# First norm of a fused three-mixer kernel: raw rows of x turned and split before the norm's factor is known, the factor applied later

## What is computed

```python
def rms_norm(x, gain):
    y = x32 * lax.rsqrt(jnp.mean(x32 * x32, axis=-1, keepdims=True) + RMS_EPS)
    return (y * gain).astype(x.dtype)

mem_n = rms_norm(mem, mem_norm_gain)
hn = rms_norm(x, g[0])
# mlstm_mixer(hn, ...)
proj = h @ w_in
q, k, v, o, gates = jnp.split(proj, ...)
gates = ML_GATE_CAP * jnp.tanh((gates + b_gate) / ML_GATE_CAP)
ig, lf = gates[..., :H], jax.nn.log_sigmoid(gates[..., H:])
...
num = einsum(s, v) + inter * (C @ q)
den = sum(s) + inter * (n . q)
h_out = num / max(abs(den), exp(-m_t))
hs = rms_norm(h_out, head_gain)
out = (hs * sigmoid(o)) @ w_out
```

## Time and profile before

| what | us |
|---|---|
| median of three runs (1288.68 to 1290.69) | 1288.76 |
| the profiled execution | 1288.84 |
| its span | 1287.1 |
| PE busy | 1273.9 |
| DVE busy | 890.5 |
| ACT busy | 695.2 |
| POOL busy | 118.0 |

### The profile page before, as it was taken

How to read it: one execution, slowest core, us unless ns; L and a number is a source line. 1 busy time by engine, 2 the same in 40 slices (tenths; PEclk the granted TensorE clock), 3 DMA queues, 4 the chain that set the end, 5 groups by cost and what they waited for, 6 DMA issues and landing times.

```text
span 1287.1 us, 17765 instructions
## 1 busy us (share of the span) xinstructions
PE 1273.9 (99%) x7337; PEld 1105.9 (86%) x7337; DVE 890.5 (69%) x1053; ACT 695.2 (54%) x976; POOL 118.0 (9%) x178
## 2 busy tenths in 40 slices
PE   7999999999999999999999999999999999999999
PEld 7888898988888988889888888898887888888887
DVE  4657775766666776877676666767785566887775
ACT  5755554644444656565554444565565654655443
POOL 7200100100000100030100000101330003100000
PEclk9999999999999999999999999999999999999999
DMA  8754644555555554354455565563544435465552
GB/s 267 261 164 145 201 162 131 184 193 196 196 193 183 182 163 132 132 176 152 152 178 195 196 196 192 168 197 99 164 163 138 157 134 194 138 214 184 187 194 98
DMA packets 156113, 223.64 MB, mean 174 GB/s; under 512 B 6103, under 2 KB 107635, under 8 KB 156032
## 3 DMA queue, kind: packets, MB, share of 16 engines
q1 hardware_dynamic: 154240, 218.18, 51.4%
q0 software_dynamic: 1664, 4.27, 1.0%
q10 hardware_dynamic: 128, 0.05, 0.0%
HBM read 221.44 MB, written 1.05 MB: 173 GB/s over the span
## 4 chain that ended last, share of the span: by engine, by line
PE 95%; DVE 2%; ACT 1%; POOL 1%; DMA 1%; issue 0%; SPq 0%; ACTq 0%
PE ps L443 18%; PE ps L496 10%; PE ps L497 10%; PE ps L498 10%; PE ps L445 9%; PE ps L426 5%; PE ps L428 5%; PE ps L427 5%; PE ps L678 5%; PE ps L680 5%; PE ps L679 5%; PE ps L517 1%; PE ps L984 1%; PE ps L461 1%; DVE wlo L1803 1%; DMA raw<-in_ml_w_in 1%
## 5 line engine op out<-in xcount | busy, mean ns | idle before, releaser
L1221 ACT ACTIVATE whi<-raw 128x1024 fp32r<-128x1024 f32 x411 | 424.4, 1052 | 314.2 <-PE ps L443 155.2
L1803 DVE TENSOR_TENSOR wlo<-raw,whi 128x1024 fp32r<-128x1024 f32 x408 | 489.2, 1229 | 140.1 <-ACT whi L1221 137.6
L443 PE MATMUL ps<-RR,whi 128*128 128x512 f32 x1024 | 354.0, 396 | 0.5 <-DVE wlo L1803 0.5
L445 PE MATMUL ps<-RR,wlo 128*128 128x256 f32 x1024 | 264.8, 279 | 0.1
L496 PE MATMUL ps<-whi,RR 128*128 128x512 f32 x592 | 236.5, 400 | 0.3 <-DVE wlo L1803 0.3
L497 PE MATMUL ps<-wlo,RR 128*128 128x512 f32 x592 | 230.9, 390 | 0.0
L498 PE MATMUL ps<-whi,RR 128*128 128x512 f32 x592 | 230.9, 390 | 0.0
L443 PEld LDWEIGHTS ps<-RR,whi 128*128 128x128 f32 x1024 | 184.9, 188 | 36.2 <-DVE wlo L1803 0.8
L445 PEld LDWEIGHTS ps<-RR,wlo 128*128 128x128 f32 x1024 | 193.0, 188 | 11.8 <-DVE RR L1834 0.4
L426 PE MATMUL ps<-RR,whi 128*128 128x256 f32 x512 | 147.1, 287 | 0.6 <-DVE RR L1834 0.5
L428 PE MATMUL ps<-RR,wlo 128*128 128x256 f32 x512 | 144.8, 283 | 0.0
(11 more groups left out here) (358 smaller groups left out, 1335.9 us busy)
## 6 DMA issues: line engine op xcount, KB each, us to landing
raw<-in_ffn_w_gate_up SPq DMA_DIRECT2D x44, 1024.0 KB, 5.1
raw<-in_ffn_w_down SPq DMA_DIRECT2D x33, 1024.0 KB, 4.9
raw<-in_w_in SPq DMA_DIRECT2D x28, 1024.0 KB, 5.0
raw<-in_ffn_w_up SPq DMA_DIRECT2D x22, 1024.0 KB, 5.1
raw<-in_xa_w_kv SPq DMA_DIRECT2D x16, 1024.0 KB, 5.2
raw<-in_sb_w_qkv SPq DMA_DIRECT2D x12, 1024.0 KB, 5.1
raw<-in_ml_w_in SPq DMA_DIRECT2D x11, 1024.0 KB, 5.7
raw<-in_xa_w_q SPq DMA_DIRECT2D x8, 1024.0 KB, 5.1
```

Of the source, the lines that this page charges most:

```text
L443: m = pe.matmul(two(ps[:, bank, :]), p.hi[:, k, :], XT2[:, k, :, :], start=k == 0, stop=k == 7)
L445: pe.matmul(ps[:, bank, 0:256], p.lo[:, k, :], X.h[:, k, :], start=False, stop=False)
L1221: act.activation(p.hi, p.raw, ACT.Copy).then_inc(S["w_hi"], 2 if p.n == pool_piece.n + 1 else 1)
L1803: dve.tensor_tensor(p.lo, p.raw, p.hi.bitcast(F32), ALU.subtract).then_inc(S["w_lo"], 2 if p.n in (2, late_piece.n + 1) else 1)
```

## The change

Raw x is turned as soon as it has landed, and the turned tiles (times the norm's gain) are split without the factor r. The projections q, k, v, o and the gates then lack r of their position. r is put in later:

- gate rows: r is turned into a row by two matmuls against the identity (bank 5), copied (`xrs`), and multiplied onto the gate rows; the bias goes into the tanh, divided by 15 (`gb15`).
- values: the copies out of PSUM are scaled by `x_rr` = r squared (r of the key, r of the value), the sigmoid of o has r as its scale, and the column of ones beside the values becomes r.
- the factor r of q is in the numerator and the denominator alike and drops out, so the bound exp(-m) is multiplied by `x_ir` = 1/r, which POOL makes as r times (mean + eps).

Pieces 0 and 1 are now halves of mlq0's rows (four feature tiles of all 256 columns each) and are loaded so, in packets twice as large. POOL casts their high parts in four halves, DVE subtracts them (`first_lo`) between the low tiles, and TensorE takes them in four quarters (`first_rows`). TensorE runs 8 products of zeros ahead of everything and 6 behind the transposes (`spin`). ACT's `squares(0)` moves behind pieces 2 and 3. DVE's `normed(0)` is gone. POOL's factors stand behind its four casts and wait for the later squares.

```diff
-            X = norm_rows(0)
-            pe.wait_ge(S["n_lo"], 2)
-            fm("mlq0", X, 4)
+            pe.wait_ge(S["w_zero"], 1)
+            spin(8)
...
+            pe.wait_ge(S["x_in0"], 16)
+            pe.wait_ge(S["x_in1"], 16)
+            for k in range(8):
+                b, half = half_bank(k, (0, 1, 2, 3))
+                for t in range(NT):
+                    m = pe.transpose(ps[:, b, 256 * half + 128 * t:256 * half + 128 * t + 128],
+                                     xr[:, t, 128 * k:128 * k + 128], ident[:, :])
+                m.then_inc(S["n_T"], 1)
+            spin(6)
+            X = Rows(XTh, XTl, S["n_lo"], [k + 1 for k in range(8)])
+            first_rows("mlq0", X, 4)
             fm("mlq1", X, 1)
+            pe.wait_ge(S["n_r"], 2)
+            for t in range(NT):
+                m = pe.matmul(ps[:, 5, 128 * t:128 * t + 128], x_r[t].to_broadcast([128, 128]), ident[:, :], start=True, stop=True)
+            m.then_inc(S["ml_r"], 1)
             gate_rows("mlg", X, 2)
...
@@ scalar_program
-            squares(0)
-            hi_to(2)
             act.wait_ge(S["gains"], 1)
             norm_hi(0, gain1(0, 0))
             hi_to(4)
+            squares(0)
...
@@ vector_program
+            def first_lo(n):
+                p, k = pieces[n // 2], slice(2 * (n % 2), 2 * (n % 2) + 2)
+                dve.wait_ge(S["hi_pool"], n + 1)
+                dve.tensor_tensor(p.lo[:, k, :], p.raw[:, k, :], p.hi[:, k, :].bitcast(F32), ALU.subtract).then_inc(S["lo_first"], 1)
+            dve.memset(Vx[:, 0, 0:256], 0.0).then_inc(S["w_zero"], 1)
             gain_columns(0)
-            normed(0)
-            lo_to(2)
-            norm_lo(0, gain1(0, 0))
+            norm_lo(0, gain1(0, 0), range(3))
+            first_lo(0)
+            norm_lo(0, gain1(0, 0), range(3, 4))
+            first_lo(1)
+            norm_lo(0, gain1(0, 0), range(4, 6))
+            first_lo(2)
+            norm_lo(0, gain1(0, 0), range(6, 8))
+            first_lo(3)
+            dve.wait_ge(S["lo_first"], 4)
             lo_to(4)
...
             for g, dst in ((32, fg), (0, ig)):
-                dve.wait_ge(S["dve_step"], step(dve.tensor_scalar(dst, ps[g:g + 4, 2, 0:256], gb[g:g + 4, 0:1], None, ALU.add)))
-                dve.tensor_tensor(dst, ps[64 + g:68 + g, 2, 0:256], dst, ALU.add).then_inc(S["ml_u"], 1)
+                dve.wait_ge(S["dve_step"], step(dve.tensor_copy(dst, ps[g:g + 4, 2, 0:256])))
+                dve.wait_ge(S["dve_step"], step(dve.tensor_tensor(dst, ps[64 + g:68 + g, 2, 0:256], dst, ALU.add)))
+                dve.tensor_tensor(dst, dst, xrs, ALU.mult).then_inc(S["ml_u"], 1)
...
@@ gpsimd_program
             pool.wait_ge(*at("mhalf", 1))
+            for p, sem in zip(pool_pieces, ("w_first", "w_raw0")):
+                pool.wait_ge(S[sem], 16)
+                for k in (0, 2):
+                    pool.tensor_copy(p.hi[:, k:k + 2, :], p.raw[:, k:k + 2, :]).then_inc(S["hi_pool"], 1)
             norm(0)
-            second = pieces[1]
-            pool.wait_ge(S["w_hi"], 2)
-            pool.tensor_tensor(second.lo, second.raw, second.hi.bitcast(F32), ALU.subtract).then_inc(S["lo_first"], 1)
+            pool.wait_ge(S["n_r"], 2)
+            for t in range(NT):
+                pool.tensor_tensor(x_rr[t], x_r[t], x_r[t], ALU.mult).then_inc(S["x_rr"], 1)
+            for t in range(NT):
+                pool.tensor_tensor(x_ir[t], x_r[t], n_st[0][t][1], ALU.mult).then_inc(S["x_ir"], 1)
             pool.affine_select(identb[:, :], identb[:, :], [[-1, 128]], ALU.not_equal, 1.0, base=0,
                                channel_multiplier=1).then_inc(S["identb"], 1)
...
             mem_norm(0)
-            pool.memset(V4[:, :, :, 256:257], 1.0).then_inc(S["v_ones"], 1)
+            for t in range(NT):
+                pool.tensor_copy(V4[:, t, :, 256:257], x_r[t].unsqueeze(1).to_broadcast([128, 4, 1])).then_inc(S["v_ones"], 1)
+            pool.wait_ge(*at("ml_em", 1))
+            pool.wait_ge(*at("x_ir", 2))
+            for t in range(NT):
+                e = emc[:, 8 * t + 4:8 * t + 8]
+                pool.tensor_scalar(e, e, x_ir[t], None, ALU.mult).then_inc(S["ml_ems"], 1)
```

More of the change, by code:

```diff
@@ L238, in build_program @@
         W = I["ml_w_in"][0]
-        fm_block("mlq", W, 0, 2)
+        chunk("mlq0", W[:, 0:256], "s")
+        chunk("mlq1", W[:, 256:512], "c")
         chunk("mlg", W[:, 3072:3080], "g")
@@ L294, in end @@
             return C[name].end
-        pool_piece = C["u2_0"].pieces[0]
+        pool_pieces = pieces[0:2] + C["u2_0"].pieces[0:1]
         late_piece = C["g2_1"].pieces[1]
@@ L332, in build_program @@
         sq = reg(9488, 512)
+        xrs = Vx[0:4, 1, 512:768]
+        gb15 = stat(2)
+        x_r = [n_st[0][t][2] for t in range(NT)]
+        x_rr, x_ir = [stat(1) for t in range(NT)], [stat(1) for t in range(NT)]
         rows = reg(7696, 1792).rearrange("p (n t) -> p n t", t=256)
@@ L417, in fm_piece @@
                 o = ps[:, bank, 256 * i:256 * i + 256]
[L418 to L421, removed]
+                pe.wait_ge(S["w_lo"], p.n + 1)
                 for k in range(8):
@@ L429, in fm_piece, with first_rows @@
                 m.then_inc(S["w_used"], 1)
+            def first_rows(name, X, bank):
+                for i, p in enumerate(C[name].pieces):
+                    for k0 in (0, 2):
+                        pe.wait_ge(S["lo_first"], 2 * i + k0 // 2 + 1)
+                        for c in range(2):
+                            o, r = ps[:, bank, 256 * c:256 * c + 256], slice(128 * c, 128 * c + 128)
+                            for k in (k0, k0 + 1):
+                                n = 4 * i + k
+                                if X.met <= n:
+                                    pe.wait_ge(X.sem, X.need[n])
+                                    X.met = n + 1
+                                pe.matmul(o, p.hi[:, k, r], X.h[:, n, :], start=n == 0 and c == 0, stop=False, skip_group_check=True)
+                                pe.matmul(o, p.hi[:, k, r], X.l[:, n, :], start=False, stop=False, skip_group_check=True)
+                                m = pe.matmul(o, p.lo[:, k, r], X.h[:, n, :], start=False, stop=n == 7, skip_group_check=True)
+                    m.then_inc(S["w_used"], 1)
             def wide(p, X, bank):
@@ L705, in feed_forward, with spin @@
                 down(NJ - 1)
+            def spin(n):
+                for i in range(n):
+                    pe.matmul(ps[:, 7, 0:128], Vx[:, 0, 0:128], Vx[:, 0, 128:256], start=True, stop=True)
+            pe.wait_ge(S["w_zero"], 1)
+            spin(8)
+            pe.wait_ge(*at("ident", 1))
             pe.wait_ge(S["g1_in"], 16)
-            pe.wait_ge(*at("ident", 1))
             pe.transpose(ps[:, 6, 0:96], grows[0:96, 0, :], ident[0:96, 0:96]).then_inc(S["gains_T"], 1)
-            X = norm_rows(0)
-            pe.wait_ge(S["n_lo"], 2)
-            fm("mlq0", X, 4)
+            pe.wait_ge(S["x_in0"], 16)
[9 more added lines that the diff above has]
+            first_rows("mlq0", X, 4)
             fm("mlq1", X, 1)
+            pe.wait_ge(S["n_r"], 2)
+            for t in range(NT):
+                m = pe.matmul(ps[:, 5, 128 * t:128 * t + 128], x_r[t].to_broadcast([128, 128]), ident[:, :], start=True, stop=True)
+            m.then_inc(S["ml_r"], 1)
             gate_rows("mlg", X, 2)
             fm("mlk0", X, 3)
-            pe.wait_ge(*at("mlq0", 1))
             fm("mlk1", X, 0)
@@ L723, in tensor_program @@
             tm("mlv0b", X, 4, 8, (1, 2))
+            pe.wait_ge(*at("mlq0", 1))
             pe.wait_ge(*at("ml_a", 1))
@@ L1835, in rest, with norm_lo @@
                                          ALU.subtract).then_inc(S[done], 1)
-            def norm_lo(no, g):
-                for k in range(8):
+            def norm_lo(no, g, tiles=range(8)):
+                for k in tiles:
                     b, half = half_bank(k, (0, 1, 2, 3))
```

85 lines of the change are left out of this document (46 added, 39 removed).

## The result

The changed kernel takes **1295.22 us** (median of 6 runs, 1294.88 to 1296.26), the kernel before 1289.09 in the same comparison: a ratio of 1.0049 [1.0039, 1.0059]. It is slower, by twice what was forecast (+3.0), and outside the range. The profiled execution took 1295.02, 6.2 more than that of before; its span is 1293.3.

The account below looks back on a forecast made before the run. TensorE, busy 1273.9 of 1287.1 us, was taken as the bound. The start's -3.2 + 0.4 was replaced by +2.3 from late GpSimd, plus +0.7: +3.0 on 1288.84 gives 1291.8 us; range 1287.0 to 1293.4.

Parts of the forecast that it names:

- The chain: Before mlv1a: later squares delay GpSimd's factors, VectorE's scalings and pieces 13 to 16, putting TensorE at +2.3 instead of -2.8.
- The start: First matmuls on TensorE: start at 9.45, mlq0 ends at 15.2 instead of 18.4, -3.2; factor row +0.4; together -2.8 us.
- the factor row: Two TensorE matmuls before the gates that turn the factors into a row: between 0.2 and 0.5, taken as +0.4 us.
- The rival of a start near 11: First matmuls: half-pace spins leave a gain of 1.0, not 2.8; 1287.8 without late GpSimd; within the 0.15 for gain carried through.
- The constants begin at 18.9, 5.8 later: GpSimd's constants: they wait for ScalarE's moved squares and the factors, so begin at 18.9, 5.8 us later than before.
- 5.1 in all, end 36.4: GpSimd's constants: selects held up by VectorE's subtractions for 5.1 us in all, moving the end from 31.3 to 36.4.
- Then 10.5 us of DMA issues: GpSimd is free at 46.9: GpSimd after its constants: 10.5 us of DMA issues follow, leaving it free at 46.9 instead of 38.07.
- Is through the 12 matmuls at 54.0: TensorE at mlv1a: asks for piece 13 at 47.2, gets it at 51.2, ends the 12 matmuls at 54.0.
- Waits for `acol` until 55.1: TensorE after the 12 matmuls: waits for `acol` until 55.1, where it passed at 52.81 before; +2.3 us.
- +0.7: TensorE at the memory gains: gain columns come 0.7 us late at a point that had 0.5 to spare.
- GpSimd later still: GpSimd's last selects: scans on the gate rows add some 2 us, free at 49, +5, 1293.8 us; chance 0.09.

Follow-up runs that it names:

- experiment 2: Changed kernel with VectorE's two scalings of the memory moved behind pieces 13 to 16, `acol` and the values' copy: 1287.54 us, ratio 0.9987.
- experiment 5: Kernel before the change with eleven memsets of 0.95 us on GpSimd ahead of its constants: 1298.08 us, ratio 1.0074.
- experiment 9: Kernel before the change with VectorE's two scalings of the memory moved behind the first copy of the values: 1288.78 us, ratio 0.9997.
- experiment 6: Changed kernel with 36 one-column memsets added in GpSimd's idle time before the first weights: 1293.51 us, ratio 1.0034.
- experiment 4: Changed kernel with 26 products of zeros on TensorE ahead of mlv1a's first tile, in its wait for piece 13: 1294.70 us, ratio 1.0043.
- experiment 1: Changed kernel with ScalarE's two squares back ahead of the turned tiles: 1289.44 us, ratio 1.0011.
- experiment 3: Changed kernel with ScalarE's squares back ahead of the tiles and VectorE's scalings of the memory behind pieces 13 to 16 and `acol`: 1286.73 us, ratio 0.9985.
- experiment 8: Changed kernel with VectorE's scalings of the memory moved later and three more products of zeros ahead of the transposes of x: 1286.41 us, ratio 0.9982.
- experiment 7: Changed kernel with squares first and scalings of the memory late, but without both spins (8 and 6): 1289.12 us, ratio 1.0000.
- experiment 10: Changed kernel with squares first, scalings of the memory late and three more spins ahead of the transposes: 1286.82 us, ratio 0.9982.

## Why the prediction had the chain right and the time wrong

**The direction and the chain were right, two terms of the sum were missing.** The chain "squares moved, constants late, selects held up, factor late, scalings late, pieces 13 to 16 late" is in the trace link by link, and experiments 2, 5 and 9 show that it is the cause: a late GpSimd alone loses at that place, and with the scalings out of the way the loss is gone.

**The start: -3.2 + 0.4 = -2.8 forecast, -2.4 measured.** The first real matmul came at 9.81 for 9.45, mlq0 ended at 15.67 for 15.2, the factor row took 0.36 for 0.4, the gate rows came at 21.79 for 21.4. The rival of a start near 11 is real too: 11.00 and 10.89 in the profiles of experiments 2 and 6. Its reason was half right, as the transposes were slow (3.65 us) and the six spins behind them were not (1.75 us and 1.68 for 1.50).

**"The constants begin at 18.9, 5.8 later": 18.35, 5.2 later. "5.1 in all, end 36.4": 36.57**, with 5.8 us of hold-ups instead of 5.1. The two deviations cancel, so the good end is partly luck. So is the sum of the hold-ups: the forecast had one select wait 2.8 us for three subtractions in a row, but in the trace selects slipped in between them and were held 0.7 to 0.9 each, and more were held elsewhere. The first took 2.02 us at 22.65, where the next of the same size took 0.65 (24.73), while VectorE ran a subtraction of 1.20 and two copies out of PSUM. The last four met the scans and small steps on the gate rows, GpSimd first and then VectorE:

```profile
24.73 0.65 POOL L2606 TENSOR_SCALAR_AFFINE_SELECT Kx<-Kx 128x64 f32<-128x64 f32 x1
...
32.78 0.63 POOL L2604 TENSOR_SCALAR_AFFINE_SELECT Kx<-Kx 128x64 f32<-128x64 f32 x1
```

```profile
32.70 0.67 DVE L2052 TENSOR_TENSOR_SCAN ar<-onesf,ar 4x256 f32<-4x256 f32 x1
```

The select ends with the scan. It and its three followers (0.44, 0.48, 0.44) take 0.24 each where nothing holds them: 1.0 us of the 5.8.

**"Then 10.5 us of DMA issues: GpSimd is free at 46.9": this step failed.** The issues took 10.5 but began 2.14 us after the cast, so GpSimd was free at 49.2. The forecast laid instructions end to end and had no term for a pause between them. Experiment 6 removes the gap and 1.7 us of time with it. This carries TensorE's piece 13 from the forecast 51.2 to 53.65: +2.4.

**"Is through the 12 matmuls at 54.0": this step failed too.** It took their 2.8 us from a TensorE that was busy. The forecast's own sum left the engine idle for 4 us ahead of them, and the measured wait was 5.76, in which the clock fell to half. They took 5.26: +2.5. A wait as short as the forecast's own would not have saved the term: in experiment 6 the clock fell in 3.54 us.

**"Waits for `acol` until 55.1" and "+0.7" for the gain columns: both absent**, since TensorE itself was now late. `acol` was ready at 57.0, TensorE asked at 58.9; the gain columns were ready at 64.96, TensorE asked at 65.50. That is -1.1 and -0.7. Experiment 4 takes the low clock away and both waits reappear, the second at 0.29.

The sum: +3.0 forecast, + 2.4 + 2.5 - 1.1 - 0.7 = **+6.1**, which is the shift of the head-0 log-decay (58.91 against 52.81). The rival "GpSimd later still" had GpSimd free at 49, which is what happened, but mostly for another reason: of its 2 us by the scans 1.0 came, inside the 5.8 above, and the 2.14 of the gap made the rest. Its time of +5 was short as well, because it had no clock term either.

Left open: why experiment 4 has two levels 1.2 us apart at the same clock, what makes three of twelve runs of experiment 1 as slow as the changed kernel, and what sets the pace of the transposes. Each kernel has one profile.

## What to carry to other kernels

A helper engine that becomes late is judged by what stands behind its consumer in the in-order queue of the next engine: moving two instructions of VectorE behind the work that TensorE waits for gave back 7.7 us, although the helper stayed as late as it was. When a forecast opens a wait on TensorE of several us, price the matmuls behind it at the lower clock, by rows that show them at that level, and drop the waits that this delay then covers. And where a long row of instructions is laid end to end, allow for a pause of some us in it, which here was 2.0 to 3.8 us in six profiles.

## What the runs showed of the hardware that was not expected

- GpSimd stops for its own instructions. The pause before the same DMA issue was 2.03 to 3.80 us in six profiles (the changed kernel and experiments 1, 2, 3, 4 and 8), 0.97 and 0.81 in experiments 7 and 10, and none after the 36 added instructions. In all eight it ends 1.7 to 2.0 us behind the one instruction packet, which passed at 36.5 to 37.9 us in the six, at the end of a weight load, and at 30.3 and 32.9 in the two. When GpSimd arrives sets only the length of the pause, not its end. When the fetch is asked for was not measured.
- A GpSimd instruction of one column can be held to the end of a whole subtraction. Two products on 128x1 took 2.06 us in experiment 1 beside VectorE's subtractions, 0.34 in the changed kernel away from them.
- A scan of VectorE on 4 partitions holds a GpSimd select as well: 0.63 us instead of 0.24, ending with the scan at 33.4.
- The 16 transposes at the start take 1.94 us (changed kernel, experiments 1, 3, 4 and 8), 2.13 (10) or 3.65 (2 and 6) behind the same eight spins (with three more in 8 and 10), and the granted clock is recorded as 1.00 in all, so the pace has to be read from the instructions there. Nor is it clear what raises the pace behind them: in the kernel before, the real matmuls start 0.5 us behind 3.68 us of transposes and come every 0.12 us, while without spins they start 1.1 us behind 3.65 us of transposes and come every 0.21 us.
